# A fourth of eight quads of gate and up weights by seven products, and the sum of a quad's four blocks by a DMA with addition

## The reference

```
h = rmsnorm(x);  proj = h @ w_in          # q, k, v, gate_b, gate_c, u
x = x + concat(diff_attention(q, k, v), gate_b * conv3(gate_c * u)) @ w_out
h = rmsnorm(x)
x = x + (silu(h @ w_gate) * (h @ w_up)) @ w_down     # hidden width 5632
```

## Time and profile before

| | |
|---|---|
| median of three runs | 2180.6 us |
| the profiled execution | 2180.93 us |
| its span | 2179.1 us |
| PE busy | 2167.8 us (99%) |
| DVE busy | 1728.6 us (79%) |
| ACT busy | 1202.9 us (55%) |
| DMA engines, mean share in the gu stage | 0.66 |

### The profile page before, as it was taken

How to read it: one execution, slowest core, us unless ns; L and a number is a source line. 1 busy time by engine, 2 the same in 40 slices (tenths; PEclk the granted TensorE clock), 3 DMA queues, 4 the chain that set the end, 5 groups by cost and what they waited for, 6 DMA issues and landing times.

```text
span 2179.1 us, 27606 instructions
## 1 busy us (share of the span) xinstructions
PE 2167.8 (99%) x10481; PEld 1808.6 (83%) x10481; DVE 1728.6 (79%) x2139; ACT 1202.9 (55%) x1646; POOL 209.3 (10%) x246
## 2 busy tenths in 40 slices
PE   9999999999999999999999999999999999999998
PEld 7888888888888888888888888888888888888886
DVE  6776676888889887788866667768988888888887
ACT  6445554655556555555544555546655555555554
POOL 0031120100000000000001311200000000000000
PEclk9999999999999999999999999999999999999999
DMA  9655455756775675667666544557567567756674
GB/s 346 208 175 173 173 171 177 224 187 207 245 224 188 221 237 193 204 223 218 224 213 202 178 163 167 181 174 223 189 230 233 194 203 244 224 182 224 213 217 179
DMA packets 131556, 449.42 MB, mean 206 GB/s; under 512 B 15072, under 2 KB 15712, under 8 KB 131040
## 3 DMA queue, kind: packets, MB, share of 16 engines
q1 hardware_dynamic: 115344, 416.40, 53.9%
q0 software_dynamic: 14784, 28.32, 7.6%
q10 hardware_dynamic: 1296, 2.94, 0.4%
HBM read 441.31 MB, written 2.10 MB: 203 GB/s over the span
## 4 chain that ended last, share of the span: by engine, by line
PE 96%; DVE 1%; ACT 1%; issue 0%; POOL 0%; DMA 0%; SPq 0%; ACTq 0%; DVEq 0%
PE bank L1674 18%; PE bank L1676 18%; PE bank L1675 18%; PE bank L1648 14%; PE bank L1651 7%; PE bank L1686 7%; PE bank L1688 7%; PE bank L1687 7%; PE bank L1839 1%; PE bank L1798 1%; PE bank L1821 1%; DVE wlo L1025 0%; PE bank L1777 0%; POOL o_rms L560 0%; PE bank L1807 0%
## 5 line engine op out<-in xcount | busy, mean ns | idle before, releaser
L628 ACT ACTIVATE whi<-raw 128x1024 fp32r<-128x1024 f32 x596 | 625.7, 1060 | 469.2 <-PE bank L1676 285.8
L1018 DVE TENSOR_TENSOR wlo<-raw,whi 128x1024 fp32r<-128x1024 f32 x596 | 724.5, 1232 | 180.9 <-ACT whi L628 167.5
L634 ACT ACTIVATE whi<-raw 128x1024 fp32r<-128x1024 f32 x368 | 343.1, 950 | 234.2 <-PE bank L1676 176.4
L1025 DVE TENSOR_TENSOR wlo<-raw,whi 128x1024 fp32r<-128x1024 f32 x368 | 390.4, 1088 | 77.1 <-ACT whi L634 75.9
L1648 PE MATMUL bank<-xg,whi 128*128 128x512 f32 x1280 | 407.0, 399 | 0.2 <-DVE wlo L1249 0.2
L1674 PE MATMUL bank<-whi,xg 128*128 128x512 f32 x1024 | 402.7, 393 | 0.0
L1676 PE MATMUL bank<-whi,xg 128*128 128x512 f32 x1024 | 399.1, 390 | 0.0
L1675 PE MATMUL bank<-wlo,xg 128*128 128x512 f32 x1024 | 398.9, 390 | 0.0
L1651 PEld LDWEIGHTS bank<-xg,wlo 128*128 128x128 f32 x1280 | 240.4, 188 | 56.9
L1651 PE MATMUL bank<-xg,wlo 128*128 128x256 f32 x1280 | 252.1, 278 | 0.0
L1676 PEld LDWEIGHTS bank<-whi,xg 128*128 128x128 f32 x1024 | 192.2, 188 | 40.3
(11 more groups left out here) (159 smaller groups left out, 2767.8 us busy)
## 6 DMA issues: line engine op xcount, KB each, us to landing
raw<-w_gu_dram SPq DMA_DIRECT2D x352, 512.0 KB, 5.2
raw<-w_in_dram SPq DMA_DIRECT2D x188, 512.0 KB, 4.5
raw<-w_down_dram SPq DMA_DIRECT2D x176, 512.0 KB, 5.3
raw<-w_out_dram SPq DMA_DIRECT2D x64, 512.0 KB, 4.4
raw<-w_gu_dram POOLq DMA_DIRECT2D x64, 256.0 KB, 6.1
raw<-w_down_dram POOLq DMA_DIRECT2D x28, 256.0 KB, 4.2
swapped<-qk POOLq DMA_DIRECT2D x32, 128.0 KB, 2.7
x_t<-x_t_dram SPq DMA_DIRECT2D x8, 256.0 KB, 6.7
```

The lines of the kernel that those rows point to most:

```text
L628: act.activation(whi[:, blk.slot(k)], raw[:, slot, half * UNIT_KT:(half + 1) * UNIT_KT, :], ACT.Copy).then_inc(hi_ready, 1)
L634: act.activation(whi[:, quad.slot(n), 0:tiles.stop - tiles.start], raw[:, quad.raw(), tiles, :], ACT.Copy).then_inc(hi_ready, 1)
L1018: dve.tensor_tensor(wlo[:, blk.slot(k)], raw[:, slot, half * UNIT_KT:(half + 1) * UNIT_KT, :], lo_bits(whi[:, blk.slot(k)]), ALU.subtract) ...
L1025: dve.tensor_tensor(wlo[:, quad.slot(n), into], raw[:, quad.raw(), tiles, :], lo_bits(whi[:, quad.slot(n), into]), ALU.subtract).then_inc( ...
```

## The change

`GU_SEVENS` goes from 3 to 4: in ten of the eleven pairs of each layer quad 3 (units 3 of both blocks) is made by seven products too. The last pair of a layer keeps its two quads. The order of such a pair becomes left 4, 5, right 4, 5, F0, F1, S0, F2, S1, left 6, right 6, F3, S2, S3, left 7, right 7; SP's, ACT's, DVE's and PE's programs are rewritten to it.

For gu quads DVE's `third_sum` goes. In its place POOL issues a second DMA with addition, from SBUF to SBUF (`add_bha`): tile 1 is added into tile 0, after `first_sum` and the quad's first split. ACT waits for it before the fourth step. The down projection keeps `third_sum`. The second batch of token sums is now of two quads instead of one. DVE's head of a four-quad pair is a new order (`four_head`); the last pair of a layer keeps `gu_head`.

```diff
-GU_SEVENS = 3
+GU_SEVENS = 4
-GU_ORDER = [("left", 3), ("left", 4), ("right", 3), ("right", 4), ("first", 0), ("first", 1), ("second", 0),
-            ("first", 2), ("left", 5), ("right", 5), ("second", 1), ("second", 2),
-            ("left", 6), ("left", 7), ("right", 6), ("right", 7)]
+GU_ORDER = [("left", 4), ("left", 5), ("right", 4), ("right", 5), ("first", 0), ("first", 1), ("second", 0),
+            ("first", 2), ("second", 1), ("left", 6), ("right", 6), ("first", 3), ("second", 2), ("second", 3),
+            ("left", 7), ("right", 7)]
...
-               "gu": [(shared_end - 4 * FORM, shared_end - 2 * FORM, 2), (shared_end - 6 * FORM, shared_end - 5 * FORM, 1)]}
+               "gu": [(shared_end - 4 * FORM, shared_end - 2 * FORM, 2), (shared_end - 8 * FORM, shared_end - 6 * FORM, 2)]}
...
+            def add_bha(quad):
+                pool.wait_ge(weights_ready, quad.split[0] + 1)
+                pool.wait_ge(first_sums, quad.number + 1)
+                pool.dma_start(raw[:, quad.raw(), 0, :], raw[:, quad.raw(), 1, :], accum_op=ALU.add
+                               ).then_inc(bha_added[quad.raw()], 16)
+            def add_four(quads):
+                for k in range(3):
+                    add_b(quads[k + 1])
+                    add_bha(quads[k])
+                add_bha(quads[3])
...
                 split_quad(quad, 2, slice(2, 4))
-                act.wait_ge(third_sums, quad.number + 1)
+                if quad.pair.name == "gu":
+                    act.wait_ge(bha_added[quad.raw()], 16 * quad.all_added)
+                else:
+                    act.wait_ge(third_sums, quad.third)
                 split_quad(quad, 3, slice(0, 2))
...
+            def four_tail(pair):                     # DVE
+                left, right = pair.blocks
+                split(left, 7, 8)
+                split(right, 7, 8)
+                gu_fold(pair)
+                gates_ups(pair, 0, 0)
...
+            def four_head(prior, pair):              # DVE
...
+                split(left, 4, 5)
+                gates_ups(prior, 0, 1)
+                split(left, 5, 6)
+                hidden_products(layer, g, 0)
+                hidden_products(layer, g, 1)
+                gates_ups(prior, 1, 0)
+                gates_ups(prior, 1, 1)
+                split(right, 4, 5)
+                hidden_products(layer, h, 0)
+                hidden_products(layer, h, 1)
+                split(right, 5, 6)
+            def gu_four(pair, prior=None):           # DVE
...
                 split_quad(q0, 0, slice(0, 2))
                 if prior is not None:
                     hidden_low(prior.layer, prior.blocks[0].i)
+                first_sum(q0)
                 split_quad(q0, 1, slice(2, 3))
-                first_sum(q0)
-                second_sum(q0)
-                third_sum(q0)
                 if prior is not None:
                     hidden_low(prior.layer, prior.blocks[1].i)
                 split_quad(q1, 0, slice(0, 2))
                 first_sum(q1)
+                second_sum(q0)
                 split_quad(q1, 1, slice(2, 3))
+                second_parts(q0)
+                split_quad(q2, 0, slice(0, 2))
                 second_sum(q1)
-                second_parts(q0)
-                first_parts(q2)
-                split(left, 5, 6)
+                split_quad(q2, 1, slice(2, 3))
+                second_parts(q1)
+                split(left, 6, 7)
                 first_sum(q2)
-                third_sum(q1)
-                split(right, 5, 6)
+                split(right, 6, 7)
+                split_quad(q3, 0, slice(0, 2))
                 second_sum(q2)
-                third_sum(q2)
-                second_parts(q1)
+                first_sum(q3)
+                split_quad(q3, 1, slice(2, 3))
+                second_sum(q3)
                 second_parts(q2)
+                second_parts(q3)
```

More of the change, by code:

```diff
@@ L166, in __init__ @@
                 q.added = plan.places[q.raw()]
+                if self.name == "gu":
+                    plan.summed[q.raw()] += 1
+                    q.all_added = plan.summed[q.raw()]
+                else:
+                    plan.thirds += 1
+                    q.third = plan.thirds
             if part in ("first", "second"):
@@ L383, in build_program @@
     b_added = [sem(f"b_added{i}") for i in range(NRAW)]
+    bha_added = [sem(f"bha_added{i}") for i in range(NRAW)]
     sum_copied = sem("sum_copied")
@@ L599, in _ @@
                 rms(2 * layer + 1)
[L600 to L603, removed]
+                add_four(plan.pairs[layer, "gu", 0].quads)
+                for p in range(1, NGU // 2 - 1):
+                    add_b(plan.pairs[layer, "gu", p].quads[0])
+                    add_four(plan.pairs[layer, "gu", p].quads)
+                for pair in (plan.pairs[layer, "gu", NGU // 2 - 1], *(plan.pairs[layer, "down", p] for p in range(2))):
+                    for quad in pair.quads.values():
                         add_b(quad)
-                for p in range(NCH // 2):
-                    for quad in plan.pairs[layer, "down", p].quads.values():
-                        add_b(quad)
+                        if pair.name == "gu":
+                            add_bha(quad)
             pool.drain()
@@ L761, in gu_head @@
                 silu(layer, right, 1)
-            def gu_three(pair, prior=None):
+            def gu_four(pair, prior=None):
                 left, right = pair.blocks
-                q0, q1, q2 = (pair.quads[k] for k in range(3))
+                q0, q1, q2, q3 = (pair.quads[k] for k in range(4))
                 act.wait_ge(raw_landed[q0.raw()][0], q0.landed())
@@ L944, in _ @@
                 left, right = pair.blocks
-                split(left, 3, 5)
+                split(left, 4, 6)
                 squares(ffn, NCH - 1)
-                split(right, 3, 5)
+                split(right, 4, 6)
                 normed(ffn, NCH - 1)
-                gu_three(pair)
-                gu_tail(pair)
+                gu_four(pair)
+                four_tail(pair)
                 for p in range(1, NGU // 2 - 1):
@@ L953, in _ @@
                     left, right = pair.blocks
-                    gu_head(prior, ((left, 3), (left, 4), (right, 3), (right, 4)))
-                    gu_three(pair, prior)
-                    gu_tail(pair)
+                    gu_head(prior, ((left, 4), (left, 5), (right, 4), (right, 5)))
+                    gu_four(pair, prior)
+                    four_tail(pair)
                 prior, pair = pair, plan.pairs[layer, "gu", NGU // 2 - 1]
@@ L960, in _ @@
                 gu_two(pair, prior)
-                gu_tail(pair)
+                two_tail(pair)
                 prior, pair = pair, plan.pairs[layer, "down", 0]
@@ L1121, in gates_ups, with four_tail, two_tail @@
                                   ).then_inc(bank_free, 1)
-            def gu_tail(pair):
+            def four_tail(pair):
+                left, right = pair.blocks
+                split(left, 7, 8)
+                split(right, 7, 8)
+                gu_fold(pair)
+                gates_ups(pair, 0, 0)
+            def two_tail(pair):
                 left, right = pair.blocks
@@ L1145, in gu_head, with gu_four @@
                 hidden_products(layer, right, 1)
-            def gu_three(pair, prior=None):
+            def four_head(prior, pair):
+                layer = prior.layer
+                g, h = (b.i for b in prior.blocks)
                 left, right = pair.blocks
-                q0, q1, q2 = (pair.quads[k] for k in range(3))
+                split(left, 4, 5)
[9 more added lines that the diff above has]
+                split(right, 5, 6)
+            def gu_four(pair, prior=None):
+                left, right = pair.blocks
+                q0, q1, q2, q3 = (pair.quads[k] for k in range(4))
                 split_quad(q0, 0, slice(0, 2))
@@ L1550, in _ @@
                     left, right = pair.blocks
-                    gu_head(prior, ((left, 3), (left, 4), (right, 3), (right, 4)))
-                    gu_three(pair, prior)
-                    gu_tail(pair)
+                    four_head(prior, pair)
+                    gu_four(pair, prior)
+                    four_tail(pair)
                 prior, pair = pair, plan.pairs[layer, "gu", NGU // 2 - 1]
@@ L1848, in gu_three @@
                 first_products(pair.quads[2])
-                plain(left, 5)
-                plain(right, 5)
                 second_products(pair.quads[1])
+                plain(left, 6)
+                plain(right, 6)
+                first_products(pair.quads[3])
                 second_products(pair.quads[2])
+                second_products(pair.quads[3])
             def gu_two(pair):
@@ L1863, in gu_two, with four_tail, two_tail @@
                 second_products(pair.quads[1])
-            def gu_tail(pair):
+            def four_tail(pair):
+                for blk in pair.blocks:
+                    plain(blk, 7)
+            def two_tail(pair):
```

(18 more changed lines are left out.)

18 lines of the change are left out of this document (11 added, 7 removed).

## The result

The changed kernel takes 2209.8 us (median; 2208.9 to 2210.5) against 2180.5: a ratio of 1.0134, interval 1.0121 to 1.0147. It is 29 us slower where 3.8 us faster was forecast, and outside the range of 2169 to 2188.

What follows compares the result with a forecast made beforehand. PE was taken to bound the kernel (96% of the chain that ended last); -13.6 + 5.8 + 1.9 + 1.2 + 0.9 = -3.8 us gave 2176.8 us against the median. The eight-in-ten range was 2169 to 2188.

Steps and rivals of the forecast that it cites:

- What was removed: PE in ten pairs of each of two layers: 24 matmuls become 21, a gain of 13.6 us.
- Step (1): S1c in each four-quad pair: ACT waits for quad 1's second sum, PE stalls 0.29 us, 5.8 us in all.
- Step (2): Quad 3's chain of load, add, sum and second add up to S3d: slack 1 us, no stall.
- Step (3): Quad 0's second add before S0d: taken as 4.1 us with 5.2 allowed, slack 1.1, cost nothing.
- rival B: Quad 0's second add lands late, delaying S0d: 0.6 us a pair, 12 us, 2189 us; chance 0.21.
- Steps (4) to (8): Tail and head, last pair, token sums, first pair: 0, 1.9, 1.2, 0.9 us; last pair's lost third sums: nothing.
- The tail and head: End of a four-quad pair and start of the next: everything just fits, cost zero, slacks of 0.1 to 0.3 us.
- The last pair's head: First transposes in each layer's last pair, which keeps gu_head: PE waits 0.94 us, twice, 1.9 us.
- The doubled token sums: Batch 1, now of two quads, delays the next split in the out block: 0.60 us, twice, 1.2 us.
- The first pair's waits: S0c in each layer's first pair, behind quad 0's second sum: 0.45 us later, twice, 0.9 us.
- Rival C: Quad 3's chain or the tail and head's thin slacks fail: 0.2 to 0.4 us a pair, 2181 to 2185; chance 0.14.

Runs made afterwards that it cites:

- Experiment 12: The kernel of experiment 9, with quad 0's sum of four blocks on DVE in all four-quad pairs instead of its second add: 2173.9 us, 0.9971.
- experiment 11: The changed kernel with only quad 3's add from DRAM made by DVE, quad 1's second sum staying where the change put it: 2189.7 us, 1.0041.
- Experiment 1: The changed kernel, but SP issues the load of left 7 and right 7 only when quad 3's add from DRAM has landed: 2193.8 us, 1.0059.
- experiment 8: The changed kernel with quad 1's second sum early on DVE and quad 3's add from DRAM made by DVE, no load held: 2176.8 us, 0.9984.
- experiment 3: The changed kernel with all third sums of gu quads back on DVE and no second adds: 2200.7 us, 1.0092.
- experiment 9: The kernel of experiment 8 with three reorderings, at the last pair's head, the first pair and the token sums: 2175.4 us, 0.9976.
- experiment 4: The kernel before (three quads, its own order), with only the third sums of gu turned into second adds by DMA: 2180.6 us, 1.0001.
- experiment 10: The kernel of experiment 8 without second adds, all third sums on DVE again: 2178.8 us, 0.9993.
- experiment 6: The changed kernel with left 7's load held until quad 3's add has landed and quad 1's second sum early on DVE: 2195.8 us, 1.0060.
- experiment 5: The changed kernel with DVE's second sum of quad 1 back ahead of quad 0's third split: 2200.5 us, 1.0089.

## Why the prediction was wrong

**What was removed: right.** 60 matmuls at 0.2267 us. Experiment 12 runs a pair in 42.0 us against 42.55, where 41.87 was the ideal.

**Step (1), S1c: right in place and mechanism, small in size.** Forecast 0.29 us; the changed kernel's S1c waited 0.3 in most pairs and 0.4 to 0.9 in six. Left out was the restart: after a wait the next matmul follows 0.33 us later instead of 0.23 (626.80 to 627.13). With it the undisturbed pairs of experiment 11 lose 0.47 us each, and the changed kernel 10.4 us in all where 5.8 was forecast.

**Step (2), quad 3's chain: the step that failed.** I wrote that the add would take "up to 5.3: T+14.1 to 15.3" beside the 1 MB load. It was issued at T+10.4, took 7.1 us and landed at T+17.5. first_sum(q3) ended at T+18.3 instead of T+16.0. I held the delay against S3d alone and found a slack of 1 us. But F3b and S2c stand behind that sum in DVE's order, and they were due before, at about T+18.8 and T+19.5. With a landing by T+15.3 both would have been split in time, so the length of the add is what failed, and the missing check of the instructions behind the sum is why nothing warned of it. The term that the sum had at 0 is 23.9 us in 20 pairs (4.4 at F3b, 19.5 at S2c), 1.3 us in the pair shown. With the 4.6 us of step (1) that is 28.5 of the 33 us between forecast and result. I had stretched the price of an add alone, 4.1 us, by 1.2 for the load beside it, and no row stood behind the 1.2. The trace of before had the row: quad 0's adds, beside loads, took 5.8 to 8.5 us there, 7.1 at the median, and the earlier trace rows showed the 8.5. Experiment 1 shows that the load is why the add is late (4.0 to 4.3 us in every pair once it is held), experiments 8 and 11 that the late add is what costs (24 and 20 us once it is gone), experiment 3 that the second adds are the lesser part.

**Step (3), the second add: near in price** (for quad 0's own 4.5 us at the median and 6.2 at most, where 4.1 was taken and 5.2 allowed; alone it takes 3.3), and its rival B wrong for this kernel: S0d waited in one of 20 pairs (0.7 us at 1631.85). It becomes real in faster kernels, in four pairs of experiment 9 by 0.7 to 1.0 us, and experiment 12 removed it.

**Steps (4) to (8).** The tail and head fit, as said, within 0.1, but left 4 comes so late that the matmul after its first follows 0.09 us late: 2 us in 20 pairs where 0 was forecast. The last pair's head cost 0.84 us where 0.94 was forecast (42.81 against 41.97 in experiment 8). The doubled token sums cost 0.6, as forecast, plus the restart. The first pair's waits grew by 0.6 and 0.4 us in the two layers, forecast 0.45.

**Rival C** named the right chain with 0.2 to 0.4 us a pair and "no change that can be told". The chain lost 1.2 us a pair, four times that. It, too, looked at the slack at the chain's end only.

## What to carry to other kernels

When a chain of load, add, sum and add is put on a queue in order, check every instruction behind the waiting one, not only the one that consumes the result. Price a DMA by rows of the same kind beside the same neighbour: here an add took 4 us alone and 6 to 9 beside a bulk load issued in the same instant. Where two edits come together, try each: the second add alone gave nothing with three quads (experiment 4), the fourth quad without it nothing that can be told (experiment 10), and the two together, in the order of the change, cost 29 us. Moving one add and one sum turned that into a gain of 4 (experiment 8).

## What the runs showed of the hardware

- An add of 256 KB from DRAM lands 4.0 to 4.3 us after its issue with no load beside it (experiment 1, 20 adds), and 5.8 to 8.6 us, 6.8 at the median, when two 512 KB loads are issued within 1.2 us of it on SP's queue (the changed kernel, 20 adds). Its first packet starts 1.6 us after the issue in the first case and 2.9 to 4.4 us in the second, while the load's start at about 1.0 us after the add's issue in the pair shown. In nine of the 20 pairs the add, half the size of either load, lands last. The Trainium skill, "DMA: Bandwidth & Descriptors", section "SWDGE vs HWDGE vs iDMA", has each DMA engine take turns between the queues that GpSimd and SP feed. The trace fits that only in part: both queues move packets later, but in the first 4.0 us after the issue at 627.90 POOL's had none and SP's 220.
- The add from SBUF to SBUF takes 3.3 us alone (quad 3's in the changed kernel, all 20). The Trainium skill, "DMA: Bandwidth & Descriptors", section "Anatomy of one DMA", has the fit 2.0 us plus bytes over 436 GB/s, which gives 2.6 us as an estimate; no add here was that quick.
- A wait of PE costs its length and another 0.1 us at the matmul after the first one (0.33 or 0.34 us apart instead of 0.23 at 626.80, 636.47 and 638.33), even where the first itself starts on time, as at 636.47.
- In experiment 6 the granted clock stood at 0.51, the lower level, for some 3 us after a wait of 2.3 us for S3d. The length of one wait does not decide it: in experiment 5 the clock fell to 0.50 at 635.0, after waits of 1.4 us at F3b and 1.1 us at S2c, and in the changed kernel waits of 1.5 and 1.1 us at the same two places (1910.46 and 1912.33) were followed by 1.00. What separates these two cases is open.
